# The fourth weight sum of each Strassen unit: an add on VectorE, or a transfer that adds to its destination

## The reference

```
h = x + 0.5 * rms(swiglu_1(rms(x)))     # (silu(x @ w_gate) * (x @ w_up)) @ w_down, d_ff = 2816
h = h + rms(mixer(rms(h)))              # pooling, sliding-window attention, short conv, gates
y = h + 0.5 * rms(swiglu_2(rms(h)))
```

## Time and profile before

| | |
|---|---|
| median of three runs | 2668.67 us |
| profiled execution | 2668.6 us, its span 2666.8 us |
| PE busy | 2638.4 us (99%) |
| DVE busy | 1708.7 us (64%) |
| ACT busy | 1072.8 us (40%) |
| POOL busy | 903.3 us (34%) |
| DMA queues with traffic | one fed by SP (205.17 MB), one by ACT (3.51 MB), two small ones that carry instructions; none by POOL |

### The profile page before, as it was taken

How to read it: one execution, slowest core, us unless ns; L and a number is a source line. 1 busy time by engine, 2 the same in 40 slices (tenths; PEclk the granted TensorE clock), 3 DMA queues, 4 the chain that set the end, 5 groups by cost and what they waited for, 6 DMA issues and landing times.

```text
span 2666.8 us, 52838 instructions
## 1 busy us (share of the span) xinstructions
PE 2638.4 (99%) x17936; PEld 2598.4 (97%) x17936; DVE 1708.7 (64%) x2592; ACT 1072.8 (40%) x1938; POOL 903.3 (34%) x730
## 2 busy tenths in 40 slices
PE   8999999999999999999999999999999999999998
PEld 7999999989999999999999999998999999999998
DVE  6888823675444788882389886166554458988612
ACT  5444613333333544461354444143333344444412
POOL 4655302140001566530256651143100035665112
PEclk9999999999999999999999999999999999999999
DMA  4232233212222222223222232232222221223221
GB/s 117 77 87 82 80 91 86 85 49 76 71 76 73 65 77 86 83 79 91 85 68 86 79 91 84 72 102 60 64 72 70 81 80 57 86 79 90 85 73 62
DMA packets 431021, 210.44 MB, mean 79 GB/s; under 512 B 44776, under 2 KB 429258, under 8 KB 430858
## 3 DMA queue, kind: packets, MB, share of 16 engines
q1 hardware_dynamic: 427252, 205.17, 26.8%
q10 hardware_dynamic: 3638, 3.51, 0.4%
HBM read 205.12 MB, written 5.29 MB: 79 GB/s over the span
## 4 chain that ended last, share of the span: by engine, by line
PE 94%; DVE 3%; issue 1%; ACT 1%; POOL 1%; DVEq 0%; ACTq 0%; POOLq 0%
PE ps L752 11%; PE ps L754 11%; PE ps L753 11%; PE ps L660 9%; PE ps L662 9%; PE ps L661 9%; PE ps L844 8%; PE ps L845 7%; PE ps L846 7%; PE ps L688 6%; PE ps L740 4%; DVE mid_lo L2004 1%; PE ps L993 1%; POOL acc_x L2379 1%; PE ps L971 1%
## 5 line engine op out<-in xcount | busy, mean ns | idle before, releaser
L2428 POOL TENSOR_TENSOR w_lo<-raw,w_hi 128x512 fp32r<-128x512 f32 x288 | 426.1, 1489 | 360.1 <-ACT w_hi L1176 358.3
L752 PE MATMUL ps<-x_r,w_hi 128*128 128x320 f32 x1728 | 534.7, 309 | 2.7 <-ACT u L1176 2.7
L754 PE MATMUL ps<-x_r,w_lo 128*128 128x320 f32 x1728 | 534.1, 309 | 0.0
L1743 DVE TENSOR_TENSOR w_lo<-raw,w_hi 128x1024 fp32r<-128x1024 f32 (+1 forms) x236 | 290.4, 1235 | 343.1 <-ACT w_hi L1184 342.9
L2379 POOL TENSOR_TENSOR acc_y<-acc_y,sq 128x320 f32<-128x320 f32 x95 | 95.2, 1002 | 1085.9 <-ACT sq L1194 1082.5
L753 PE MATMUL ps<-x_r,w_hi 128*128 128x320 f32 x1440 | 445.1, 309 | 0.0
L844 PE MATMUL ps<-mid_hi,w_hi 128*128 128x320 f32 x1408 | 438.6, 312 | 1.4 <-DVE mid_lo L2004 1.4
L845 PE MATMUL ps<-mid_lo,w_hi 128*128 128x320 f32 x1408 | 435.2, 309 | 0.0
L846 PE MATMUL ps<-mid_hi,w_lo 128*128 128x320 f32 x1408 | 435.1, 309 | 0.0
L1184 ACT ACTIVATE w_hi<-raw 128x1024 fp32r<-128x1024 f32 (+1 forms) x244 | 248.9, 1026 | 462.2 <-PE ps L846 293.9
L660 PE MATMUL ps<-x_r,w_hi 128*128 128x320 f32 x1088 | 345.4, 317 | 0.0
(11 more groups left out here) (229 smaller groups left out, 5082.7 us busy)
## 6 DMA issues: line engine op xcount, KB each, us to landing
raw<-in_ffn_w_gate_dram SPq DMA_DIRECT2D x352, 128.0 KB, 2.3
raw<-in_ffn_w_up_dram SPq DMA_DIRECT2D x352, 128.0 KB, 2.3
raw<-in_ffn_w_down_dram SPq DMA_DIRECT2D x348, 128.0 KB, 2.2
raw<-in_w_in_dram SPq DMA_DIRECT2D x304, 128.0 KB, 2.3
raw<-in_w_branch_dram SPq DMA_DIRECT2D x64, 128.0 KB, 2.6
raw<-in_w_out_dram SPq DMA_DIRECT2D x64, 128.0 KB, 2.3
raw<-in_ffn_w_down_dram SPq DMA_DIRECT2D x68, 64.0 KB, 1.9
rows<-in_x_prompt_dram SPq DMA_DIRECT2D x4, 512.0 KB, 5.8
```

The costliest lines, as they stand in the source:

```text
L752: pe.matmul(bank(b), wh, lhs(0, k), start=begin and k == 0, stop=False, skip_group_check=True)
L754: mm = pe.matmul(bank(b), wl, lhs(0, k), start=False, stop=k == QK - 1, skip_group_check=True)
L1743: dve.tensor_tensor(w_cols(1, hi_slot, 0, nk), raw_cols(raw_slot, 0, nk), f32(w_cols(0, hi_slot, 0, nk)), ALU.subtract).then_inc(w_split, 1)
L2428: pool.tensor_tensor(w_cols(1, slot, k0, k0 + QK), src, f32(w_cols(0, slot, k0, k0 + QK)), ALU.subtract).then_inc(ws_lo, 1)
```

## The change

The add that makes T4 leaves VectorE's list. GpSimd issues a transfer in its place, from r0's low half (which then holds T2) onto r0's high half, and the transfer adds to what is there. It has a semaphore of its own, `t4_made`, on which ScalarE's copy of T4 waits; the count of `t_made` goes from four to three for each unit. In GpSimd's list it stands behind low B22 and ahead of low T2, and it waits until T2 is made; in the first unit of a feed-forward it is ahead of low T2 too.

```diff
-                    act.wait_ge(t_made, t0 + at * 4 + made)
+                    if what == "T4":
+                        act.wait_ge(t4_made, at * 16 + 16 * b20 + 16)
+                    else:
+                        act.wait_ge(t_made, t0 + at * 3 + made)
...
                     dve.tensor_tensor(raw_cols(r0, 0, QK), t_one[:, :], raw_cols(r1, QK, KD), ALU.subtract).then_inc(t_made, 1)
-                    dve.wait_ge(t_made, t0 + at * 4 + 3)
-                    dve.tensor_tensor(raw_cols(r0, QK, KD), raw_cols(r0, QK, KD), raw_cols(r0, 0, QK), ALU.add).then_inc(t_made, 1)
...
+                def fourth_sum(u, at):
+                    r0 = 2 * (u % 2)
+                    pool.wait_ge(t_made, t0 + at * 3 + 3)
+                    alone(pool)
+                    pool.dma_start(raw_cols(r0, QK, KD), raw_cols(r0, 0, QK), accum_op=ALU.add).then_inc(t4_made, 16)
+
                 def unit_low(u, at):
-                    for j, what in enumerate(("B22", "T2", "T1", "T3", "T4")):
-                        t_low(what, u, at * 5 + j + 1)
+                    t_low("B22", u, at * 5 + 1)
+                    fourth_sum(u, at)
+                    for j, what in enumerate(("T2", "T1", "T3", "T4")):
+                        t_low(what, u, at * 5 + j + 2)
```

More of the change, by code:

```diff
@@ L220, in trunk_kernel @@
         w0_hi, w0_lo = sem("w0_hi"), sem("w0_lo")
-        t_made = sem("t_made")
+        t_made, t4_made = sem("t_made"), sem("t4_made")
         ws_hi, ws_lo = sem("ws_hi"), sem("ws_lo")
@@ L1241, in ffn @@
                 g = l * GROUPS + FFN_GROUP0[n]
-                b20, p0, t0 = per_ffn(l, n, UNITS), per_ffn(l, n, PRODS), per_ffn(l, n, 4 * UNITS)
+                b20, p0, t0 = per_ffn(l, n, UNITS), per_ffn(l, n, PRODS), per_ffn(l, n, 3 * UNITS)
                 a0, ss0, s30, d0 = (per_ffn(l, n, c) for c in (QK, SUMS3, QK, QK))
@@ L1289, in t_high @@
                                            "T3": (2, raw_cols(2 * (u % 2) + 1, 0, QK), 2, 0),
-                                           "T4": (4, raw_cols(2 * (u % 2), QK, KD), 2, QK)}[what]
-                    act.wait_ge(t_made, t0 + at * 4 + made)
+                                           "T4": (None, raw_cols(2 * (u % 2), QK, KD), 2, QK)}[what]
+                    if what == "T4":
+                        act.wait_ge(t4_made, at * 16 + 16 * b20 + 16)
+                    else:
+                        act.wait_ge(t_made, t0 + at * 3 + made)
                     act.wait_ge(*used)
@@ L1871, in t_second @@
                     dve.wait_ge(w0_lo, b20 + at + 1)
-                    dve.wait_ge(t_made, t0 + at * 4 + 1)
+                    dve.wait_ge(t_made, t0 + at * 3 + 1)
                     dve.tensor_tensor(raw_cols(r0, 0, QK), t_one[:, :], raw_cols(r1, QK, KD), ALU.subtract).then_inc(t_made, 1)
-                    dve.wait_ge(t_made, t0 + at * 4 + 3)
-                    dve.tensor_tensor(raw_cols(r0, QK, KD), raw_cols(r0, QK, KD), raw_cols(r0, 0, QK), ALU.add).then_inc(t_made, 1)
                 def done(what, at):
@@ L2401, in ffn @@
             def ffn(n, l, sm):
-                ss0, ws0 = per_ffn(l, n, SUMS3), per_ffn(l, n, 5 * UNITS)
+                ss0, ws0, t0 = per_ffn(l, n, SUMS3), per_ffn(l, n, 5 * UNITS), per_ffn(l, n, 3 * UNITS)
                 m0, h0 = per_ffn(l, n, NF), hi0(l, n)
@@ L2439, in ffn @@
                     sums12_low(k)
+                fourth_sum(0, 0)
                 for j, what in enumerate(("T2", "T1", "T3", "T4")):
```

## The result

The changed kernel took 2727.11 us (median of four runs, 2725.85 to 2727.98) against 2668.22 for the kernel before on the same chip: ratio 1.0221, interval 1.0204 to 1.0237, 58.9 us more. The forecast was 39.8 us more. The profiled execution of after took 2726.89 us, its span is 2725.1.

A forecast was written before the change was run, and what follows sets the result against it. The prediction took TensorE, busy 99% of the span, as the bound. Nothing gained from the lighter VectorE, plus 9.95 us of ScalarE delay four times (39.8 us) on 2668.6, gave 2708 us; range 2667 to 2810.

The forecast's parts named there:

- the likeliest case: Transfer's landing delays ScalarE's copy of T4, L from 3.1 to 4.4 us: 2671 to 2759 us, chance 0.47.
- the list: ScalarE's in-order list: a late copy of T4 holds up the next unit's `w0_high`; 16 L - 49.3 us per feed-forward.
- the tail: After a feed-forward's last unit: the late copy of T4 adds L - 2.80 us, and its unbroken chain delays TensorE.
- What the issue itself takes of GpSimd: GpSimd's time per transfer issue ahead of low T2: between 0.37 and 1.49 us, taken as 0.95; low sums shift some 0.2.
- What is added on ScalarE: the step that decides: Copy of T4 waits for the landing, delaying `w0_high` unit by unit: 9.95 us per feed-forward, 39.8 us in all.
- L: Time from T2's end until ScalarE's copy of T4 can start, forecast at 3.65 us.
- the forecast's own rule: Delay per feed-forward from units and tail is 17 L - 52.1 us, passed to TensorE four times.
- runs shorter than its rows: Sign of being wrong: L over 3.1 us yet no gaps on TensorE, the ScalarE-VectorE unit loop being faster than traced.
- What would make D smaller: All `w0_low` short on VectorE (1.23, not 2.31 us): 0.5 us gained a turn, limit 3.08 to 3.6; not counted on.
- Hidden: Rival: transfer lands in 2.6 us while ScalarE would wait for TensorE anyway; 2668.6 us, chance 0.22.
- Slow transfer: Rival: landing takes 3.6 us plus 1.49 on GpSimd, L 5.1; 2807 us, deciding from L 4.4 up; chance 0.24.
- GpSimd as the bound: Rival: over 4.8 us per issue makes GpSimd's work exceed a unit; at 6 us, 2755 us; chance 0.04.

The follow-up runs named there:

- the third experiment: Changed kernel plus a one-column GpSimd memset behind the transfer's issue and a wait for its end ahead of low T2: 2691.96 us, ratio 1.0091 to the kernel before.

## Why the forecast came out on the right side by the wrong step

The time lies in the range and near the middle of the likeliest case's, by luck: the part of the sum that was priced, the list and the tail, is worth 24.9 us at most when it stands alone (the third experiment) and not 39.8, and most of the 58.9 come from a cost that stands nowhere in the prediction.

**The step that failed** is the costing of GpSimd's issue: "What the issue itself takes of GpSimd" was put at 0.95 us and its harm at a shift of low T2 by some 0.2 us. The duration was right (0.88 us), and low T2 started at 164.52, 1.28 us after T2's end where it had been 0.74. What was missing is what the issue does to the passes behind it: one of VectorE's small ops beside them takes 5.07 to 5.76 us, 64 times in the 72 units. Curing that takes away 34.0 of the 58.9 us (the third experiment); of the rest the list is worth 18.7, and 6.1 are left, the tail's wait among them.

How it comes about is shown as far as this: an issue, or an op on 16 partitions, ahead of a chain of four passes makes VectorE wait for the whole chain; with an op on all partitions that is waited for VectorE waits for one pass only (which of the two does it, the op or the wait, no run tells apart). That GpSimd's parts then run apart through the chain, so that at no moment all of them pause, is an inference; in its favour are, behind an issue, the second pass that starts 0.35 us before the first ends, and the memset that starts before the issue's end (174.44 against 174.74) and ends after it (174.86). In the kernel with the 16-partition op the records of the passes overlap by 0.04 us only, so this can't be read from their lengths alone.

The Trainium skill would have pointed there. "GPSIMD Engine Reference", section "Instruction dispatch", says that consecutive GpSimd instructions are no barrier between its eight cores, each of which serves 16 partitions and goes on to the next instruction when its own share is done; section "When to use GPSIMD" has a pair of the cores prepare a transfer. The trace agrees: low T2 starts at 164.52, 0.26 us before the issue ends. The Trainium skill, "SBUF — State Buffer", section "Who interferes with whom", has a VectorE instruction with two SBUF inputs contend with a GpSimd instruction that reads SBUF. The waits beside the passes agree; that such a wait can last over four instructions the Trainium skill doesn't say there, and the runs show over 5 us of it.

**"What is added on ScalarE: the step that decides"** did not decide. Its sign came (63 waits for the DMA ahead of the copy), and L was 4.08 us: 0.67 from T2's end to the issue, 3.3 from issue to landing, 0.11 to the copy. The forecast had 0.95 + 2.6 for issue and landing together, a little too much, and 0.1 for two semaphores, a term without a row, where 0.67 + 0.11 was measured. By the forecast's own rule that would have been 17 x 4.08 - 52.1 = 17.3 us for each feed-forward, 2738 us. That after came close to it is chance: with the stall, VectorE comes to `w0_low` 2.9 us later than ScalarE allows it at this odd unit's end (0.6 at the even one), and the copy can be moved without effect. The case that the prediction itself named as a refutation, L over 3.1 and a loop that "runs shorter than its rows", is what the third experiment shows: with L of 4.28 us at an even unit's end (173.13 to 177.41) and 4.02 at an odd one (186.03 to 190.05) the loop costs 21 us in the units, where the rule gives 4 x (16 x 4.08 - 49.3) = 64 already for 4.08. From `w0_low`'s start to T2's end it was 6.28 and 6.56 us there, not 6.9 and 7.2. That is the gain under "What would make D smaller", which the forecast left out, but not by its reason alone: `w0_low` took 1.72 and 1.34 us in place of 1.23 and 2.31, 0.48 less in two units, and the other 0.8 came from the small products, one of which took 0.49 in place of 1.61.

**What held:** removing 49.8 us from VectorE gave nothing back, even where the stall was cured; GpSimd did not become the bound (34% busy); the tail pays for the landing, if only some 1.5 us.

**The rivals.** Hidden: no. Slow transfer: no, L was 4.08 us, under the 4.4 from which it was to decide. GpSimd as the bound: no. None of them named VectorE being held up by GpSimd, though the earlier trace rows had its price at small scale. The prediction took the long `w0_low` (2.31 us) for the one beside GpSimd's passes; GpSimd's line before the change shows passes beside both:

```profile
162.57 3.05 POOL L2428 TENSOR_TENSOR w_lo<-raw,w_hi 128x512 fp32r<-128x512 f32 x2
...
175.12 3.85 POOL L2428 TENSOR_TENSOR w_lo<-raw,w_hi 128x512 fp32r<-128x512 f32 x2
```

The long one starts at 164.40, inside a pass, and ends 1.09 us after that pass (165.62 to 166.71). The short one (176.59, 1.23 us) starts as a pass ends, and the next pass pays: these two take 0.80 us more than the two of 162.57. Here whichever comes second waits for one instruction of the other.

## What to carry to other kernels

Price a transfer that GpSimd issues by the GpSimd passes behind it and by VectorE's ops beside those, not by its own 0.88 us. Behind an issue, or behind an op on 16 partitions, ahead of a chain of passes, a one-column op on all 128 (at most 0.43 us) and a wait for its end gave 34 to 163 us back here. A sum that comes near the measured time is no proof of its mechanism: the run that took the named wait away, and changed nothing, was.

## What the runs showed of the hardware

- One op of GpSimd on 16 of 128 partitions, 1.28 us long, ahead of four passes made the kernel 6.2% slower; the same op with a memset of one column behind it, 0.3%.
- An adding transfer from SBUF to SBUF, issued by GpSimd, landed 3.3 us after its issue for 256 KB and 2.2 us for 32 KB; the issue took 0.88 us in both.
- VectorE's op on two SBUF tiles ran at its usual 0.49 us beside GpSimd's issue.
- Beside a chain of passes with no such op or issue ahead of it, VectorE's op on two SBUF tiles waited for one pass and took 1.11 us (160.35, before the change); behind an issue it took 5.59.
